# Start addresses in SBUF: the operands of the products moved to multiples of 512 bytes

## The reference, cut to what matters

```python
def hybrid_layer(x, ...):                      # twice
    h = rmsnorm(x, pre_mix_g)
    proj = h @ w_in                            # 1024 -> 7,440 columns in 11 parts
    y_a = deltanet_branch(...) @ w_up_dn       # conv, gated delta rule over chunks, 8 heads
    y_b = swa_sink_branch(...) @ w_up_sw       # sliding window attention, 16 heads of 64
    mix = (sigmoid(gate_a) * y_a + sigmoid(gate_b) * y_b) @ w_o
    x = x + rmsnorm(mix, post_mix_g)
    ff = square(relu(rmsnorm(x, pre_mlp_g) @ w_ff1)) @ w_ff2    # 1024 -> 4096 -> 1024
    return x + rmsnorm(ff, post_mlp_g)

def second_block(x, ...):                      # once
    proj = rmsnorm(x, norm_g) @ w_in + b_in
    ya = s5_branch(ua, ...) * silu(za)         # state space scan, then a gate by w_glu
    yb = pool_branch(ub, ...) * silu(zb)
    merged = sigmoid(ga) * (ya @ w_branch_a) + sigmoid(gb) * (yb @ w_branch_b)
    return rmsnorm(x + merged @ w_out, final_norm_g)
```

## Time and profile before

| | |
|---|---|
| median of 3 runs | 2455.24 us (2446.15 to 2457.42) |
| the profiled execution, its own time | 2449.71 us |
| its span, first to last instruction | 2447.9 us |
| mean granted clock of TensorE | 0.985 |
| busy: PE, PEld | 97%, 77% of the span |
| busy: DVE, ACT, POOL | 51%, 44%, 47% |
| DMA | 207.31 MB, 85 GB/s on the mean |

### The profile page before, as it was taken

The page is one execution under the profiler, slowest core; times in us unless marked ns, Lnnn a source line. Parts: engine busy times, 40 slices in busy tenths (PEclk is TensorE's granted clock), DMA queues, the critical chain, the costliest instruction groups (busy, mean ns, idle before and its releaser), DMA issues.

```text
span 2447.9 us, 33347 instructions
## 1 busy us (share of the span) xinstructions
PE 2365.6 (97%) x12948; PEld 1877.2 (77%) x12948; DVE 1255.8 (51%) x2460; ACT 1071.2 (44%) x2284; POOL 1154.4 (47%) x848
## 2 busy tenths in 40 slices
PE   7999999999999999989999999999999999899998
PEld 5777777778778888867878777787777788777876
DVE  4877864663341111168777546633496511565153
ACT  6566553443343323245665434433533332434442
POOL 4333234334666556453334333356665564544464
PEclk9999899999999999999999999999999999999999
DMA  4211112222222222222111121223224332374222
GB/s 141 68 61 52 44 53 69 70 70 78 95 71 94 94 95 95 95 69 70 53 52 61 44 78 61 70 86 107 67 95 134 122 101 92 103 199 119 95 87 78
DMA packets 76510, 207.31 MB, mean 85 GB/s; under 512 B 16704, under 2 KB 27712, under 8 KB 75840
## 3 DMA queue, kind: packets, MB, share of 16 engines
q1 hardware_dynamic: 76352, 205.18, 26.1%
HBM read 194.66 MB, written 10.49 MB: 84 GB/s over the span
## 4 chain that ended last, share of the span: by engine, by line
PE 82%; DVE 9%; ACT 3%; POOL 2%; issue 2%; DMA 1%; SPq 1%; DVEq 0%; ACTq 0%; POOLq 0%
PE ps L970 24%; PE ps L971 22%; PE ps L972 22%; PE ps L1979 1%; PE ps L1991 1%; PE ps L1907 1%; PE ps L1930 1%; POOL wL L933 1%; PE ps L1926 1%; DVE ctw L1186 1%; PE ps L1985 1%; ACT wH L926 1%; ACT prob L1449 1%; DVE ctmp L1186 1%; PE ps L1956 1%
## 5 line engine op out<-in xcount | busy, mean ns | idle before, releaser
L933 POOL TENSOR_TENSOR wL<-raw,wH 128x512 fp32r<-128x512 f32 x660 | 903.2, 1390 | 1068.1 <-ACT wH L926 1068.0
L926 ACT ACTIVATE wH<-raw 128x512 fp32r<-128x512 f32 x660 | 379.6, 623 | 752.9 <-PE ps L972 748.8
L970 PE MATMUL ps<-hH,wH 128*128 128x512 f32 x1592 | 665.4, 418 | 1.7 <-POOL wL L933 1.7
L971 PE MATMUL ps<-hL,wH 128*128 128x512 f32 x1592 | 631.2, 396 | 0.0
L972 PE MATMUL ps<-hH,wL 128*128 128x512 f32 x1592 | 631.1, 396 | 0.0
L970 PEld LDWEIGHTS ps<-hH,wH 128*128 128x128 f32 x1592 | 301.5, 189 | 73.9 <-issue 8.9
L972 PEld LDWEIGHTS ps<-hH,wL 128*128 128x128 f32 x1592 | 300.4, 189 | 73.2
L971 PEld LDWEIGHTS ps<-hL,wH 128*128 128x128 f32 x1592 | 301.8, 190 | 58.0 <-issue 0.7
L970 PE MATMUL ps<-OH,wH 128*128 128x512 f32 x576 | 230.9, 401 | 4.8 <-DVE acc L1786 1.8
L971 PE MATMUL ps<-OL,wH 128*128 128x512 f32 x576 | 227.9, 396 | 0.0
L972 PE MATMUL ps<-OH,wL 128*128 128x512 f32 x576 | 227.9, 396 | 0.0
(11 more groups left out here) (411 smaller groups left out, 3394.6 us busy)
## 6 DMA issues: line engine op xcount, KB each, us to landing
raw<-w SPq DMA_DIRECT2D x345, 512.0 KB, 3.4
mats<-matsD SPq DMA_DIRECT2D x4, 1408.0 KB, 6.8
x<-xT SPq DMA_DIRECT2D x8, 256.0 KB, 6.7
matsD<-Cd SPq DMA_DIRECT2D x8, 256.0 KB, 2.7
matsD<-wide SPq DMA_DIRECT2D x4, 512.0 KB, 3.5
mats<-lagsD SPq DMA_DIRECT2D x32, 64.0 KB, 6.2
outT<-acc SPq DMA_DIRECT2D x8, 256.0 KB, 2.2
matsD<-tab SPq DMA_DIRECT2D x8, 128.0 KB, 1.9
```

Source lines behind the costliest of these rows:

```text
L926: act.activation(weights_at(slot)[0][:, k, :], raw[:, n % RAW, k, :], ACT.Copy).then_inc(high_done, 1)
L933: pool.tensor_tensor(low[:, k, :], raw[:, n % RAW, k, :], high[:, k, :].bitcast(F32), ALU.subtract).then_inc(low_done, 1)
L970: pe.matmul(out, wh, rH[:, t, :], start=(t == 0), stop=False)
L971: pe.matmul(out, wh, rL[:, t, :], start=False, stop=False)
```

## The change

Two fillers are allocated that nobody uses: one ahead of `x`, one ahead of `ropeC`, each as large as it takes to bring the next address to a multiple of 512. Three small tables (`par2`, `spare`, `first_gain`) are allocated ahead of the second filler and no longer behind `wL`. All else moves because of these. No instruction is added, taken away or moved on any engine.

```diff
+        def even(name):
+
+            rest = -((nc.sbuf_base + 31) // 32 * 32) % 512
+            if rest:
+                sb(f"even_{name}", [P, rest // 4])
+
         TILE = SEQ * 4
+        even("x")
         x = sb("x", [P, KT, SEQ])
         hH, hL = sb("hH", [P, KT, SEQ], F32R), sb("hL", [P, KT, SEQ], F32R)
         cst = sb("cst", [P, NCONST])
         par = sb("par", [P, DEPTH, NPARAM])
+        par2 = sb("par2", [P, NPARAM2])
+        spare = sb("spare", [P, 1])
+        first_gain = sb("first_gain", [P, KT])
+        even("rope")
         rope_at = (nc.sbuf_base + 31) // 32 * 32
         ropeC, ropeS = sb("ropeC", [P, SEQ]), sb("ropeS", [P, SEQ])
         raw = sb("raw", [P, RAW, KT, P])
         wH, wL = sb("wH", [P, SPLIT, KT, P], F32R), sb("wL", [P, SPLIT, KT, P], F32R)
-        par2 = sb("par2", [P, NPARAM2])
-        spare = sb("spare", [P, 1])
-        first_gain = sb("first_gain", [P, KT])
         rstd, rstdp = sb("rstd", [P, SEQ]), sb("rstdp", [P, SEQ])
```

## The result

The change made the kernel faster: 2415.33 us median of 4 runs (2411.91 to 2423.19) against 2455.1 us before (4 runs too); the ratio of the means is 0.985 with a 95% interval of 0.9815 to 0.9884. The forecast was no effect, 2452 us and not under 2440. It was wrong: the time came out near the forecast's first rival, but by another cause than that rival names.

The account below looks back on a forecast made before the run. TensorE, busy 97% of the span, was taken as the bound. Terms: 0 on PE, 0 on hidden engines, 0 ± 2.2 us on DMAs, so 2452 us, between profiled 2449.7 and median 2455.2; range 2440 to 2463.

Parts of the forecast that it names:

- first rival: Matmul products: every start off a multiple of 512 costs the same; removing it gives 2285 us, or 2409 at 5 ns; chance 0.12.
- the relation of the two operands: Matmuls: moving start minus stationary start, 288 and 480 modulo 512 before, 0 after; same pitch at both, so effect 0.
- the slots at 320: Weight blocks xwH and xwL, used mostly at layer seams: can't be read finely, show no large step; counted 0.
- The moving operand and the stationary one by themselves: Matmuls: the start address of the moving tile or of the weight block taken alone changes the pitch by 0.
- The second rival: Matmuls and buffers all starting in step modulo 512 collide, raising the pitch: 41 us slower, 2491 us; chance 0.08.
- ScalarE, GpSimd, VectorE and the DMAs: Other engines' operations and transfers: 0 each; DMA waits of 18.4 us at 12% give 2.2 us either way.
- The rule of the Trainium skill: SBUF is read in 16-byte lines and only a new line costs; starts are already multiples of 32, so no effect.

Follow-up runs that it names:

- The sweep: TensorE-only kernels streaming fp32r matmuls of 512 columns, m - s (moving start minus stationary start, modulo 256) varied: 226.7 ns at 0 and 240, 228.9 at 64, 233.3 at 224.

## Why the prediction was wrong

**The step that failed** is the one on the relation of the two operands: it noted 288 and 480 for m - s before and 0 after, found the same pitch at both, and argued that 480 "is only 32 bytes from 0", so 0 as well. The sweep shows a function that isn't smooth. 288 is 32 modulo 256 and 480 is 224, both are 233.3 ns, and so are 96 and 192; the gain is at 0 and 16 below it, with a smaller one at 64. Two points of before on the same high level were read as proof that there is no other level. In place of the 0 stand 6.7 ns x 7400 products in close succession, 49 us, less 8 us because the short stretches gain less than that, less 5 us of grown waits.

The trace of before could have told. The prediction set the slots at 320 (`xwH`, `xwL`) aside as not to be read finely, because their group means hold waits and a lower clock, said that "they show no large step", and left their relation, 64 modulo 256, out of its list. Single matmuls in order of time show five undisturbed tiles of them at 228.7 to 229.0 ns beside neighbours at 233.3. That is a step of 4.5 ns, clear of the 0.5 ns a product that its range allowed. It would not have given the size, but it speaks against a pitch that doesn't feel the addresses.

**The moving operand and the stationary one by themselves**: 0 each was right. The kernel with all else but the weights at 0 gained nothing (0.9999), and with both operands at 320 or 352 the pitch is at its lowest, 226.7 ns. The multiples of 512 of the change are a way to bring operands in step, not the cause.

**The first rival** had the right place (the surplus of 20 ns in the pitch at the high clock), a wrong mechanism (the absolute start) and a price three times too high: of the 20 ns 6.7 went. Its other price, 5 ns a product, 41 us and 2409 us, comes near the 41.1 us that the steps lost, but no row gave that 5 ns; that is luck. Its argument against itself, that 128 and 320 had the same pitch, was sound against the absolute start, and said nothing on the relation. Of the remaining 13.3 ns bf16 has 2.5 too; the other 10.9 come with fp32r, and what they are stays open. The chance of 0.12 was too low for a case in which an unexplained surplus stood in 79% of the span and the new state was in no row.

**The second rival** was the reverse of what happens: being in step is what helps at 512 columns. At 256 it did hurt, 120.0 against 113.3 ns in one run and against 117.8 in the other.

**ScalarE, GpSimd, VectorE and the DMAs** at 0 held. The splits take 624 and 1392 ns against 623 and 1390, the weights land in 3.3 us and not 3.4, and PE waited 9.2 us for the constants and not 9.4. The table `bc`, whose 3.0 us the prediction set against the weights' 3.4, took 3.3 after the change, so the 12% read from the two rows didn't come with the new addresses.

**The rule of the Trainium skill** on 16-byte lines ("SBUF — State Buffer", "Door 1") would give no effect for starts that are all multiples of 32. The measurement differs and decides: streams at multiples of 32 range from 226.7 to 234.2 ns.

What stays open is the mechanism. Shown are the relation modulo 256, its independence of the absolute start, and that, of the types and clocks tried, only fp32r at the high clock has it. That moving reads and weight loads collide in the memory is only an idea: the narrower weight loads, which should then have paid less, paid as much, and float32, whose loads are as long, doesn't feel the starts.

## What to carry to other kernels

Where long runs of fp32r matmuls with 512 columns bound a kernel, place the moving and the stationary buffers at equal distances over a multiple of 256 bytes, all of them, high and low parts alike; here that took 3% off the pitch and 1.5% off the kernel, for two fillers. In bf16 and float32 it was worth nothing at the starts tried, and for other widths of fp32r it must be measured. And a surplus in the bounding engine's pitch that no row explains is a reason for a wider range: equal readings at two settings don't show that a third is equal. Before calling a setting unseen or unreadable, look for it in the view of single instructions: a group's mean can hide a clean stretch of it.

## What was not expected of the hardware

- fp32r matmuls in a stream settle into a repeating rhythm: before, mostly steps of 232 and 235 ns in turn; after, 227, 227, 226; at m - s = 64, 226, 229, 232; at 128, 229 and 238. The two means seen most are whole numbers of cycles of 1.2 GHz: 272 for 226.7 ns, 280 for 233.3.
- The same relation can have two rhythms: at 128, with 233.3 ns in one sweep and 232.3 in another, and in the kernel with the weights alone at 0 five long stretches over `hH` at 232.4 and two at 233.3; at 192 with 256 columns, 113.3 and 117.8.
- bf16 shows neither: 215.8 ns at every start.
